# Values by seven products, and experts with their combination as one stage, in a two-block transformer kernel

## What is computed

```python
proj = h @ w_in                                   # h: (1024, 1024), w_in: (1024, 3*1024 + 16)
q, k, v, f_pre = jnp.split(proj, [D, 2 * D, 3 * D], axis=-1)
q = rms_norm(q.reshape(B, S, N_HEADS, HEAD_DIM), q_g)
k = rms_norm(k.reshape(B, S, N_HEADS, HEAD_DIM), k_g)
v = v.reshape(B, S, N_HEADS, HEAD_DIM)
log_f = jax.nn.log_sigmoid(f_pre + b_f)
F = jnp.cumsum(log_f, axis=1)
...
# second block: each token goes to two of 32 experts
hid = jax.nn.silu(xb @ exp_gate[e]) * (xb @ exp_up[e])
y = (hid @ exp_down[e]) * wgt[:, None]
...
ffn = zeros.at[row_tok].add(ys)                   # two weighed rows for each token
return layer_norm_2(DEEPNORM_ALPHA * h + ffn, ln2_g, ln2_b)
```

## Time and profile before

| | us |
|---|---|
| median of three runs | 3013.24 |
| lowest and highest | 3011.2, 3014.5 |
| the profiled execution | 3023.13 |
| its span, from first to last instruction | 3021.4 |
| TensorE busy, share of the span | 2836.5, 94% |
| projection of q and k (75.03 to 270.38) | 195.35 |
| projection of v, busy | 110.0 |
| last expert's copy to the next stage's first work | 2950.07 to 2963.5 |

### The profile page before, as it was taken

The page is one execution under the profiler, slowest core; times in us unless marked ns, Lnnn a source line. Parts: engine busy times, 40 slices in busy tenths (PEclk is TensorE's granted clock), DMA queues, the critical chain, the costliest instruction groups (busy, mean ns, idle before and its releaser), DMA issues. The chain is left out here.

```text
span 3021.4 us, 48468 instructions
## 1 busy us (share of the span) xinstructions
PE 2836.5 (94%) x18832; PEld 1851.9 (61%) x18832; DVE 1538.4 (51%) x4129; ACT 725.1 (24%) x1635; POOL 265.6 (9%) x343
## 2 busy tenths in 40 slices
PE   4999989999999999999999999999999896999996
PEld 3886456664588544886444777777777554444442
DVE  5543056771355566655564666666666466111115
ACT  3211055551210000000002344444444200111111
POOL 0000011100000000000000122222222100010002
PEclk7999999999999999999999999999999897999998
DMA  5010033321022453224443100000000121999965
GB/s 224 29 47 38 0 105 99 108 83 42 14 84 84 167 181 139 84 86 162 161 177 144 57 25 26 2 26 16 12 25 2 50 87 43 351 358 352 355 242 195
DMA packets 103937, 338.62 MB, mean 112 GB/s; under 512 B 6944, under 2 KB 16672, under 8 KB 94640
## 3 DMA queue, kind: packets, MB, share of 16 engines
q1 hardware_dynamic: 96816, 310.55, 28.6%
q0 software_dynamic: 6912, 25.17, 2.3%
HBM read 302.60 MB, written 33.10 MB: 111 GB/s over the span
## 5 line engine op out<-in xcount | busy, mean ns | idle before, releaser
L1854 PE MATMUL mixing_ps<-all_main,pre_ws 128*128 128x256 f32 x1152 | 315.5, 397 | 0.0
L1189 PE MATMUL mlp_ps<-mlp_w2s,all_main 128*128 128x512 f32 x512 | 239.6, 592 | 0.0
L2790 PE MATMUL ex_pg<-all_main,ex_xT 128*128 128x512 f32 x512 | 226.9, 596 | 0.0
L1854 PEld LDWEIGHTS mixing_ps<-all_main,pre_ws 128*128 128x128 f32 x1152 | 200.0, 189 | 30.3
L1189 PE MATMUL mlp_ps<-all_main 128*128 128x512 f32 x384 | 183.2, 593 | 0.7 <-DVE all_main L1402 0.7
L2790 PEld LDWEIGHTS ex_pg<-all_main,ex_xT 128*128 128x128 f32 x512 | 98.0, 192 | 123.3 <-issue 123.3
L1189 PEld LDWEIGHTS mlp_ps<-mlp_w2s,all_main 128*128 128x128 f32 x512 | 96.6, 190 | 117.8 <-issue 104.6
L2180 POOL TENSOR_TENSOR all_tail<-all_tail,pre_cst 128x256 f32<-128x256 f32 x120 | 103.6, 878 | 430.5 <-DVE all_tail L2236 290.0
L1189 PEld LDWEIGHTS mlp_ps<-all_main 128*128 128x128 f32 x384 | 72.6, 190 | 93.4 <-issue 68.5
L2924 DVE TENSOR_TENSOR ex_hid<-ex_pg,ex_sil 128x256 f32<-128x256 f32 x32 | 13.6, 425 | 223.8 <-ACT ex_sil L2872 223.8
L1139 PE MATMUL mlp_ps<-all_main,all_early 128*128 128x256 f32 x512 | 121.0, 379 | 0.0
(11 more groups left out here) (440 smaller groups left out, 5039.8 us busy)
## 6 DMA issues: line engine op xcount, KB each, us to landing
mlp_w2s<-in_w SPq DMA_DIRECT2D x64, 1024.0 KB, 4.9
all_main<-in_w_gu SPq DMA_DIRECT2D x32, 2048.0 KB, 9.3
all_early<-in_w SPq DMA_DIRECT2D x32, 1024.0 KB, 4.9
att_wa<-in_w_ada SPq DMA_DIRECT2D x32, 512.0 KB, 3.7
all_early<-in_w_d SPq DMA_DIRECT2D x16, 1024.0 KB, 10.9
all_main<-in_w_d SPq DMA_DIRECT2D x16, 1024.0 KB, 11.2
y_rows<-ex_y SPq DMA_DIRECT2D x32, 512.0 KB, 3.0
qkv_wq<-in_w_qkv SPq DMA_DIRECT2D x6, 2048.0 KB, 7.7
```

What stands on the lines that cost most here:

```text
L1189: last = nc.tensor.matmul(ps[:, PRODUCTS.index(name), :], lhsT=lhsT, rhs=rhs, start=j == 0, stop=j == FPAIRS - 1)
L1854: last = nc.tensor.matmul(ps[:, bank, 0:UT], lhsT=ws[:, n, k, :], rhs=xT[:, k, (col + NB) % S:(col + NB) % S + UT], start=(k == 0), stop=( ...
L2790: last = nc.tensor.matmul(pg[:, n % 2, :], lhsT=xT[:, n % 2, k, :], rhs=gu[n][:, k, :], start=(k == 0), stop=(k == KT - 1))
```

## The change

1. `stage_qkv` takes all six chunks with seven products. The squares, and what follows from them, stay with the first four (`NORMED = 4`); the root and the inverse of the norms are taken in the fifth chunk. Restoring `hT` falls away. The sums S1 to T2 move from `main` to `xres` (`sums`), since v's columns of `main` now are written while the sums are still in use.
2. x is therefore lost in `xres`, and SP loads it again in `stage_attention`, at the third of the eight pairs (`p == 3`), behind that turn's four ada rows and ahead of the wait for `maxed`.
3. `wf` and `fb` are loaded by `stage_start`, behind its last slice of w_ada.
4. `stage_experts` and `stage_combine` become `stage_experts_combine`. The LayerNorm rows are loaded, the diagonals made and h multiplied by alpha (in place) at its start, on VectorE ahead of everything else. The gathers of the y rows wait only for the stores. TensorE weighs the rows without the alpha product. VectorE adds h with one instruction that also sums along the row, takes the mean from that, and shifts and multiplies by the gain in one instruction; ScalarE squares the centred row (`Square` with a bias) with its sum and takes the root; VectorE multiplies by the inverse and adds the offset.

```diff
+                sp.dma_start(wf[:], w_f).then_inc(wf_in, 16)
+                sp.dma_start(fb[:], b_f.rearrange("(h a) -> h a", a=1)).then_inc(wf_in, 16)
...
-    SEVENTHS = 4
+    NORMED = 4
...
-        S1, S2, S4 = ([main[:, 2 * n + k // 2, 2 * D + (k % 2) * NB:2 * D + (k % 2 + 1) * NB] for k in range(HK)] for n in range(3))
+        S1, S2, S4 = ([sums[:, 2 * n + k // 2, (k % 2) * NB:(k % 2 + 1) * NB] for k in range(HK)] for n in range(3))
         T1, T2, T4 = (t.rearrange("p (k c) -> p k c", k=HK) for t in
-                      (main[:, 6, 2 * D:3 * D], main[:, 7, 2 * D:3 * D], gates[:, 0, :]))
+                      (sums[:, 6, :], sums[:, 7, :], gates[:, 0, :]))
...
-                sp.dma_start(wf[:], w_f).then_inc(wf_in, 16)
-                sp.dma_start(fb[:], b_f.rearrange("(h a) -> h a", a=1)).then_inc(wf_in, 16)
...
-                for c in range(SEVENTHS):
+                for c in range(CHUNKS):
...
-                pe.wait_ge(part, part_at(SEVENTHS - 1, 2, "c12"))
-                for c in range(SEVENTHS, CHUNKS):
-                    pe.wait_ge(w_in[c % 2], 16 * (c // 2 + 1))
-                    for t in range(TT):
-                        m = (c - SEVENTHS) * TT + t
-                        if m == 1:
-                            pe.wait_ge(part, 28 * SEVENTHS)
-                        if m == 4:
-                            pe.wait_ge(restored, 1)
-                        if m >= 8:
-                            pe.wait_ge(v_taken_a, m // 2 - 3)
-                            pe.wait_ge(v_taken_v, m // 2 - 3)
-                        for k in range(KT):
-                            last = nc.tensor.matmul(ps[:, m % 8, :], lhsT=hT[:, k, t * P:(t + 1) * P], rhs=wq[:, c % 2, k, :],
-                                                    start=(k == 0), stop=(k == KT - 1))
-                        last.then_inc(v_mm, 1)
...
-                        for name in SQUARES:
-                            squares(c, i, name)
+                        if c < NORMED:
+                            for name in SQUARES:
+                                squares(c, i, name)
...
+                        if c == NORMED and i == 0:
+                            act.wait_ge(prep, 1)
+                            nc.scalar.activation(norm, norm, ACT.Sqrt).then_inc(root, 1)
...
+                        if c == NORMED and i == 0:
+                            inverse_norms()
...
-                for k in range(HK):
-                    last = tt(A21[k], A11[k], A21[k], ALU.subtract)
-                last.then_inc(restored, 1)
...
-                for m in range(0, 2 * TT, 2):
-                    c, t = SEVENTHS + m // TT, m % TT
-                    dve.wait_ge(v_mm, m + 1)
-                    nc.vector.tensor_copy(main[:, t, c * QN:(c + 1) * QN], ps[:, m % 8, :]).then_inc(v_taken_v, 1)
...
+                    if c + 1 == NORMED:
+                        mean_squares()
+                dve.wait_ge(part, 28 * CHUNKS)
...
+                    if p == 3:
+                        for half in range(2):
+                            sp.dma_start(xres[:, half * TT // 2:(half + 1) * TT // 2, :],
+                                         x[half * NB:(half + 1) * NB, :].rearrange("(t p) d -> p t d", p=P)).then_inc(x_back, 16)
...
+        yg = room.rearrange("p (r c) d -> p r c d", c=2)
+        mv = s.sb("mv", [P, TT, 4])
+        eps = s.sb("eps", [P, 1])
+        ps = s.ps("ps", [P, 2 * RING, NB])
+        px, pg, ph, py = (ps[:, 2 * n:2 * n + 2, :] for n in range(4))
...
+                for n in range(2):
+                    sp.dma_start(rows[:, n, :], ln_rows[n].partition_broadcast(P)).then_inc(r_in, 16)
...
+                for t in range(TT):
+                    sp.wait_ge(ready, t + 1)
+                    sp.dma_start(out_rows[t * P:(t + 1) * P, :], hres[:, t, :]).then_inc(stored, 16)
+                sp.wait_ge(stored, 16 * TT)
...
+                for n in range(2):
+                    pool.wait_ge(y_out[n], 16 * (EXPERTS // 2 + 1))
+                pool.sem_inc(gate, 1)
+                for t in range(TT):
+                    if t >= RING:
+                        pool.wait_ge(summed, t - RING + 1)
+                    for c in range(2):
+                        nc.gpsimd.indirect_dma_start(out=yg[:, t % RING, c, :], out_offset=None, in_=y_dram,
+                                                     in_offset=bass.IndirectOffsetOnAxis(ap=dest[:, c, t:t + 1], axis=0)
+                                                     ).then_inc(g_in[t % RING], 16)
...
+                def weigh_rows(t):
+                    pe.wait_ge(g_in[t % RING], 32 * (t // RING + 1))
+                    if t >= RING:
+                        pe.wait_ge(added, t - RING + 1)
+                    for half in range(2):
+                        for c in range(2):
+                            last = nc.tensor.matmul(ps[:, 2 * (t % RING) + half, :], lhsT=diag[:, c, t, :],
+                                                    rhs=yg[:, t % RING, c, half * NB:(half + 1) * NB], start=(c == 0), stop=(c == 1))
+                    last.then_inc(summed, 1)
...
+                pe.wait_ge(weighed, 2 * TT)
+                for t in range(TT):
+                    weigh_rows(t)
...
+                for t in range(TT):
+                    act.wait_ge(centre, t + 1)
+                    if t >= 2:
+                        act.wait_ge(squared, t - 1)
+                    nc.scalar.activation(xT[:, t % 2, :, :].rearrange("p a b -> p (a b)"), hres[:, t, :], ACT.Square, bias=mv[:, t, 1:2],
+                                         accum_out=mv[:, t, 2:3]).then_inc(squared, 1)
+                    act.wait_ge(squared, t + 1)
+                    nc.scalar.activation(mv[:, t, 3:4], mv[:, t, 2:3], ACT.Sqrt, bias=eps[:], scale=1.0 / D).then_inc(rooted, 1)
...
+                def finish(t):
+                    dve.wait_ge(rooted, t + 1)
+                    nc.vector.reciprocal(mv[:, t, 3:4], mv[:, t, 3:4]).then_inc(inverse, 1)
+                    dve.wait_ge(inverse, t + 1)
+                    dve.wait_ge(shifted, t + 1)
+                    nc.vector.scalar_tensor_tensor(out=hres[:, t, :], in0=y[:, t % 2, :], scalar=mv[:, t, 3:4], in1=rows[:, 1, :],
+                                                   op0=ALU.mult, op1=ALU.add).then_inc(ready, 1)
+
+                for t in range(TT):
+                    for c in range(2):
+                        nc.vector.tensor_scalar(diag[:, c, t, :], ident[:], wgt[:, c, t:t + 1], None, ALU.mult).then_inc(weighed, 1)
+                nc.vector.memset(eps[:], LN_EPS).then_inc(scaled, 1)
+                for t in range(TT):
+                    nc.vector.tensor_scalar(hres[:, t, :], hres[:, t, :], ALPHA, None, ALU.mult).then_inc(scaled, 1)
...
-def stage_combine(nc, room, hres, y_dram, dest, wgt, ln_rows, out_rows, ident):
...
+                    nc.vector.tensor_tensor_reduce(out=hres[:, t, :], in0=ps[:, 2 * (t % RING):2 * (t % RING) + 2, :].rearrange("p a b -> p (a b)"),
+                                                   in1=hres[:, t, :], scale=1.0, scalar=0.0, op0=ALU.add, op1=ALU.add,
+                                                   accum_out=mv[:, t, 0:1]).then_inc(added, 1)
+                    dve.wait_ge(added, t + 1)
+                    nc.vector.tensor_scalar(mv[:, t, 1:2], mv[:, t, 0:1], -1.0 / D, None, ALU.mult).then_inc(centre, 1)
+                    dve.wait_ge(centre, t + 1)
+                    if t >= 2:
+                        dve.wait_ge(ready, t - 1)
+                    nc.vector.scalar_tensor_tensor(out=y[:, t % 2, :], in0=hres[:, t, :], scalar=mv[:, t, 1:2], in1=rows[:, 0, :],
+                                                   op0=ALU.add, op1=ALU.mult).then_inc(shifted, 1)
```

More of the change, by code:

```diff
@@ L118, in modulation_columns, with stage_start @@
     dve.wait_ge(finished, 3)
-def stage_start(nc, x, cols1, w_ada, xres, main, modc, cols, silu, hT, ones, ident):
+def stage_start(nc, x, cols1, w_ada, w_f, b_f, xres, main, modc, cols, silu, hT, wf, fb, wf_in, ones, ident):
     HT = TT // 2
@@ L252, with stage_qkv @@
 QN = 512
-def stage_qkv(nc, hT, w_qkv, w_f, b_f, qk_gain, main, ss, f_rows, gates, norm, gain):
+def stage_qkv(nc, hT, wf, fb, wf_in, w_qkv, qk_gain, main, sums, ss, f_rows, gates, norm, gain):
     CHUNKS = QKV // QN
-    SEVENTHS = 4
+    NORMED = 4
     HK, HN = KT // 2, QN // 2
@@ L287, in order @@
             return LAST_PAIR if i == 3 else PRODUCTS
-        steps = [(c, i, name) for c in range(SEVENTHS) for i in range(4) for name in order(i)]
+        steps = [(c, i, name) for c in range(CHUNKS) for i in range(4) for name in order(i)]
         mm_at = {key: n + 1 for n, key in enumerate(steps)}
```

173 lines of the change are left out of this document (42 added, 131 removed).

## The result

Two comparisons with the kernel before were timed. In the first the changed kernel took 2985.4 us (median of 4 runs, 2983.9 to 2989.0) against 3013.9: ratio 0.9908, 95% interval 0.9891 to 0.9925. In the second it took 2987.6 (5 runs) against 3012.9: ratio 0.9910, 0.9896 to 0.9925. That is 28.5 and 25.3 us; forecast were 31.9 us and 2981.3, with 2974 to 2992 as the range.

The account below looks back on a forecast made before the run. TensorE, busy for 94% of the span, was taken as the bound, except in the final combination and at stage edges. Terms 12.2 + 4.8 + 0 - 1.5 + 16.4 = 31.9 us, from the median 3013.24, gave 2981.3 us; range 2974 to 2992.

Parts of the forecast that it names:

- Term 1: Projection of q, k and v: the values' two chunks with seven products instead of eight, 12.2 us gained.
- Term 2: Gate's weights loaded a stage earlier: TensorE starts 1.8 us sooner, its clock holds for 3.0 more, 4.8 us gained.
- Term 3: Attention: loading x again stays hidden, 0 us; bounds 0 and -3 us.
- Term 4: Front of the experts: LayerNorm rows ahead of the first token gather delay it, -1.5 us; VectorE's added work hidden.
- The rival that priced it at 5.7 us: Front of the experts: VectorE's wide multiplications hold up the gathers, up product 5.7 us late, total 2985.5 us; chance 0.10.
- Term 5: Combination merged into the experts' stage: earlier gathers and weighing, then VectorE bound at 4.0 us a tile, 16.4 us gained.
- It starts at 2963.0: Combination: TensorE, after its empty overflow loop, starts the first weighing at 2963.0 instead of 2971.65.
- The base: Whole kernel: gains subtracted from the median 3013.24 us, the profiled execution's 10 us excess taken to lie outside the changed places.
- GpSimd last through its loop: Combination: GpSimd reaches the old stage edge last, so gathers go out late and term 5 shrinks by 8, 2989; chance 0.08.
- A chain of 4.8 us a tile: Combination: VectorE's chain takes 4.8 us a tile, total 2987 us; chance 0.10.
- The clock falling during the added products: Values' chunks: TensorE's clock falls to 1.2 GHz, costing 97.7 us if throughout, total 3079; slower-kernel chance 0.01.

Follow-up runs that it names:

- sync_shift: The changed kernel with 24 more waits on an already raised semaphore in SyncE's program, ahead of its overflow loop; profiled span 2979.9 us.

## Why the prediction came out

**Term 1, 12.2: right.** 1344 records, a clock of 1.00, 12.15 us between these traces, no engine but TensorE near its limit.

**Term 2, 4.8: right in kind, at the upper end in size.** TensorE starts earlier, 1.7 us after the start of its last transpose instead of 3.6, with all gate records at full clock. The gain is 4.8 us against the profile I read and 3.7 against the second one, where the clock was low for half as long. One execution's fall was taken as the kernel's.

**Term 3, 0: right**, 0.1 at most. The load is asked for at 432.49, 68.9 us after attention's first record, where the forecast 449 was 67.5 after it. The ada row behind it is asked for at 441.36, lands 12.9 us later, and VectorE uses it at 456.25: 2 us of reserve, for which I had 3. So it is hidden, but by little.

```profile
432.49 2.04 SPq L627 DMA_DIRECT2D all_xres<-in_x  x2
...
441.36 8.70 SPq L624 DMA_DIRECT2D att_wa<-in_w_ada  x2
```

**Term 4, -1.5: mis-sized.** The first turn of x is 0.8 us late, not 1.5: I took the gather's 6.03 us from the earlier trace rows, where eight gathers and the rows ran together. And of the 0.8 only 0.1 to 0.4 is left at the end of the stage, since the clock's rise does not shift with the start. Beside the wide multiplications of 0.65 us GpSimd loses 0.25 us on a gather's issue and 0.33 on a copy. The Trainium skill, "SBUF — State Buffer", section "Who interferes with whom", says that a VectorE operation in a two-port mode and a GpSimd operation lock each other out for a whole instruction. No delay here is longer than one multiplication, and no run shows whether that lock is its cause. The rival that priced it at 5.7 us fails, since the second gather's issue takes 0.97 as before, and TensorE turns the third x only at 2560.0, 20 us after its gather's issue. The trace before had a sign of this that I misread: I set the issue of 1.06 us beside the narrow diagonals against 1.15, the first of its row, and saw no blocking. The next one, issued as VectorE's diagonals end, takes 0.94:

```profile
2965.48 1.06 POOL L3012 DMA_INDIRECT all_main<-y_rows,all_dest  x1 [0.30 <-issue]
2966.85 0.94 POOL L3012 DMA_INDIRECT all_main<-y_rows,all_dest  x1 [0.30 <-issue]
```

**Term 5, 16.4: mis-sized by 3.4.** Measured are 13.0 us (last copy to VectorE's last pass 68.3 us before, 55.3 after; 13.1 between the second profiles). The step that failed is "It starts at 2963.0", 12.9 us after the copy; it starts after 15.9 and 16.4. That TensorE's loop is the limit was right, and so was its length, 12.96 wherever the slow instructions are absent; with them absent (sync_shift) the stretch from the copy to the end falls by 16.1 to 16.6, the term as predicted. What follows the start was right: 39.4 us to VectorE's last pass against 38.9, the first weighing at a clock of 0.50, then 4.04 us a tile, for which 4.0 was said. From the copy to the first gather it was 4.2 us, for 4.

**The base.** I subtracted from the median, not from the profile, as the profiled execution was 10 us above it "outside these places". That was right in the main; the second profile shows it, attention and the stages from the MLP to routing being the places. But 1.1 of the 11.6 us lay in term 2's own place.

**Rivals.** GpSimd last through its loop: it gathers 4.2 us after the copy, so no. A chain of 4.8 us a tile: 4.04. The clock falling during the added products: 1.00 throughout.

Sum with the measured sizes: at least 12.15 + 3.7 - 0.1 - 0.4 + 13.0 = 28.4 us, at most 12.15 + 4.8 - 0.1 + 13.0 = 29.8, against 28.5 and 25.3 measured. The first comparison came out 3.4 us short of the forecast 31.9, about what the slow instructions took from term 5 (2.9 to 3.4). That it is so near is in part luck: term 4 cost 1.1 to 1.4 us less than I had, and term 2 gave up to 1.1 less, and the two cancel. The second is 3 us shorter still; its interval (22 to 31 us) takes that in, and the 1.3 us in attention left open above may be part of it.

## What to carry to other kernels

- Profile the kernel before twice. Here one profile had 11.6 us more than the other, nearly all in stages that nobody touched, and a term read from one execution's clock was 1.1 us larger than by the other.
- An empty loop on the engine that is waited for is work: 15 turns at 0.74 us stood on the critical path, before the change and after it. A test around the loop gave 5.9 to 6.3 us, beside the 13.0 of the merge itself. About 3 of them are the turns (from the copy to the end 52.4 us, against 55.2 to 55.5 in the programs that pass the turns without slow instructions), and the rest are the slow instructions.
- A delay should be priced at the end of its stage, not where it arises: of 0.8 us at the experts' start only 0.1 to 0.4 was left there, since the clock rose at its own moment, while the 3 us at the first weighing's start stayed in full.

## What had not been expected of the hardware

- While GpSimd's gathers of 0.5 MB ran, single register and branch instructions on four other engines' queues took 0.70 us each instead of 0.03 to 0.25, a dozen or more within 9 us, in each of three profiles of two programs. With 24 more idle waits in SyncE's program they were absent in its one profile. The cause is open.
- A granted clock of 0.50 appeared for 3.4 to 17.1 us at the start of attention, in different lengths in two executions of one program, and moved that stage by up to 4 us.
- VectorE's 128x1024 multiplication by a constant took 0.65 us, and lengthened GpSimd's issue of a gather from 0.97 to 1.22 us.
